# Feed-forward input projections: two 256-column matmuls on the same weights become one of 512 columns, and the halves are added outside TensorE

## The reference

```python
FFN_HIDDEN = 2816

def _swiglu(h, w_in, w_out):
    gate, up = jnp.split(h @ w_in, 2, axis=-1)
    return (jax.nn.silu(gate) * up) @ w_out

def _sublayer(x, fn, mod_j, g, b, weight):
    shift, scale, gate = mod_j[:, 0, None, :], mod_j[:, 1, None, :], mod_j[:, 2, None, :]
    y = fn(x * (1 + scale) + shift)
    return _layernorm(DEEPNORM_ALPHA * x + weight * gate * y, g, b)
```

## Time and profile before

| | |
|---|---|
| median of 3 runs | 3108.59 us (3104.44 to 3113.85) |
| the profiled execution | 3112.86 us |
| its span (first to last instruction) | 3111.0 us |
| TensorE busy | 2752.4 us, 88% of the span |
| VectorE busy | 1968.1 us, 63% |
| ScalarE busy | 1237.7 us, 40% |
| GpSimd busy | 1422.2 us, 46% |
| granted TensorE clock, mean | 0.913 of full speed |

### The profile page before, as it was taken

One profiled execution on the slowest core, in us unless ns is written; L12 is line 12 of the kernel. 1 busy time (PEld: TensorE's weight loads), 2 busy tenths in 40 slices (PEclk: granted clock), 3 DMA queues, 4 the chain that ended last, 5 costly groups with the idle time before them and its releaser, 6 DMA issues.

```text
span 3111.0 us, 49422 instructions
## 1 busy us (share of the span) xinstructions
PE 2752.4 (88%) x20583; PEld 2600.7 (84%) x20583; DVE 1968.1 (63%) x2280; ACT 1237.7 (40%) x1358; POOL 1422.2 (46%) x1126
## 2 busy tenths in 40 slices
PE   3998789999976999999789999999779979779797
PEld 3998679999965999998764999999669968468797
DVE  5657766676658666656766765766765454754553
ACT  2444444444444444434232444444444334334342
POOL 0890949579293692984730098494550000000000
PEclk7998989999987999999865999999889989789898
DMA  7765558667462675866620486675535535033452
GB/s 267 267 245 161 190 176 267 214 226 265 162 238 82 214 269 178 266 241 200 207 83 1 160 273 236 211 262 203 187 108 178 187 133 175 24 99 131 139 177 108
DMA packets 357173, 576.21 MB, mean 185 GB/s; under 512 B 22255, under 2 KB 297898, under 8 KB 356906
## 3 DMA queue, kind: packets, MB, share of 16 engines
q1 hardware_dynamic: 357034, 574.29, 54.2%
HBM read 573.20 MB, written 1.05 MB: 185 GB/s over the span
## 4 chain that ended last, share of the span: by engine, by line
PE 71%; DVE 13%; POOL 5%; ACT 4%; issue 4%; DMA 3%; SPq 1%; POOLq 0%; DVEq 0%; ACTq 0%
PE ps L1663 59%; PE ps L1716 3%; POOL mod_acc L647 3%; ACT whi L674 2%; PE ps L1722 1%; PE ps L2051 1%; POOL mod_w L642 1%; DVE wlo L1040 1%; DMA raw<-in_ffn_w_in_dram 1%; PE ps L2042 1%; DVE conv L1479 1%; PE ps L1773 1%; DVE z L1201 1%; DVE z L1179 1%; DMA raw<-in_ssm_w_in_dram 1%
## 5 line engine op out<-in xcount | busy, mean ns | idle before, releaser
L1040 DVE TENSOR_TENSOR wlo<-raw,whi 128x2048 fp32r<-128x2048 f32 x387 | 978.6, 2532 | 657.0 <-ACT whi L674 655.6
L1663 PE MATMUL ps<-H_hi,whi 128*128 128x256 f32 x3840 | 1099.4, 286 | 60.2 <-DVE conv L1479 21.8
L1663 PE MATMUL ps<-H_lo,whi 128*128 128x256 f32 x3840 | 1094.4, 285 | 0.0
L1663 PE MATMUL ps<-H_hi,wlo 128*128 128x256 f32 x3840 | 1094.0, 285 | 0.0
L674 ACT ACTIVATE whi<-raw 128x2048 fp32r<-128x2048 f32 (+1 forms) x402 | 759.9, 1892 | 645.6 <-DMA raw<-in_ffn_w_in_dram 259.7
L1663 PEld LDWEIGHTS ps<-H_hi,whi 128*128 128x128 f32 x3840 | 745.3, 194 | 68.6 <-issue 40.9
L647 POOL TENSOR_TENSOR mod_acc<-mod_acc,mod_w 128x512 f32<-128x512 f32 x450 | 793.0, 1788 | 0.0
L1663 PEld LDWEIGHTS ps<-H_lo,whi 128*128 128x128 f32 x3840 | 745.5, 194 | 0.2
L1663 PEld LDWEIGHTS ps<-H_hi,wlo 128*128 128x128 f32 x3840 | 745.1, 194 | 0.0
L1663 PE MATMUL ps<-A_hi,whi 128*128 (+1 forms) x1880 | 537.1, 286 | 21.0 <-DVE wlo L1040 21.0
L1663 PE MATMUL ps<-A_hi,wlo 128*128 (+1 forms) x1880 | 534.9, 285 | 0.0
(11 more groups left out here) (318 smaller groups left out, 2777.2 us busy)
## 6 DMA issues: line engine op xcount, KB each, us to landing
raw<-in_ffn_w_in_dram SPq DMA_DIRECT2D x176, 1024.0 KB, 5.3
mod_w<-in_w_mod_dram SPq DMA_DIRECT2D x180, 768.0 KB, 5.3
raw<-in_ffn_w_out_dram SPq DMA_DIRECT2D x88, 1024.0 KB, 4.8
raw<-in_w_gate_up_dram SPq DMA_DIRECT2D x22, 1024.0 KB, 5.1
raw<-in_ssm_w_in_dram SPq DMA_DIRECT2D x20, 1024.0 KB, 6.9
raw<-in_w_in_dram SPq DMA_DIRECT2D x14, 1024.0 KB, 5.1
raw<-in_diff_w_in_dram SPq DMA_DIRECT2D x12, 1024.0 KB, 7.7
raw<-in_w_down_dram SPq DMA_DIRECT2D x11, 1024.0 KB, 4.8
```

Of the source, the lines that this page charges most:

```text
L1040: tt(wlo[b % RAW][:, r], raw[b % RAW][:, r], whi[b % RAW][:, r].bitcast(F32), ALU.subtract).then_inc(w_lo, 1)
L1663: m = pe.matmul(out, l, r, start=first and i == 0, stop=last and i == 2, skip_group_check=rest)
```

## The change

In the input projection of all nine feed-forward parts, `columns` is replaced by `wide`. `H_hi` and `H_lo` become the two halves of one tile `H_two`. One matmul of 512 columns (a whole bank) multiplies `whi` by both: whi x H_hi goes to columns 0 to 255 of the bank and whi x H_lo to columns 256 to 511. The matmul wlo x H_hi stays one of 256 columns and adds to the first half. So 16 x 3 matmuls in a block become 16 x 2. Blocks 0 and 1, in `opening`, keep their three matmuls of 256 columns, the third now writing to the second half.

The two halves of a bank must then be added. ScalarE copies the second halves to SBUF (`low_part`, into `sg` or `am`), VectorE adds the first halves (`add_halves`), and only this addition frees the banks. Silu now runs on `sg` in SBUF, one turn later, and the product of gate and up has both inputs in SBUF. The output projection and all other stages are as before.

```diff
+        H_two = at("H_two", [P, 2, DC, S], o_hh, F32R)
+        H_hi, H_lo = H_two[:, 0], H_two[:, 1]
...
                 def gate(i, it=None):
 
                     p = g.p + i
+                    v = plan.free_val[p]
+                    act.wait_ge(banks_free[p % 2], v if it is None else 2 * it + v)
+                    nc.scalar.activation(sg[:, i // 2 % 2], sg[:, i // 2 % 2], ACT.Silu).then_inc(s["gated"], 1)
+
+                def low_part(i, it=None):
+                    j, p = i // 2, g.p + i
+                    reader, dst = (("multiplied", sg), ("a_lo", am))[i % 2]
+                    if j >= 2:
+                        v = n[reader] + j - 1
+                        act.wait_ge(s[reader], v if it is None else 2 * it + v)
                     u = g.l + 2 * (i + 1)
                     act.wait_ge(products, u if it is None else 8 * it + u)
-                    nc.scalar.activation(sg[:, i // 2 % 2], ps[:, bank(p):bank(p) + 2, 0:S], ACT.Silu)\
-                        .then_inc(banks_free[p % 2], 1)
+                    copy(dst[:, j % 2], ps[:, bank(p):bank(p) + 2, S:2 * S]).then_inc(s["low_out"], 1)
...
                 def turn(i, it=None):
                     convert(g.b + i + 2, it)
-                    if i % 2 == 0:
-                        gate(i, it)
+                    if i % 2 == 1:
+                        gate(i - 1, it)
+                    low_part(i, it)
                     if i % 2 == 0 and i >= 2:
                         product_hi(i // 2 - 1, it)
...
+                def add_halves(dst, i, it):
+
+                    p = g.p + i
+                    v = n["low_out"] + i + 1
+                    dve.wait_ge(s["low_out"], v if it is None else 4 * it + v)
+                    tt(dst, dst, ps[:, bank(p):bank(p) + 2, 0:S], ALU.add).then_inc(banks_free[p % 2], 1)
+
                 def product(j, it=None):
-
+                    add_halves(am[:, j % 2], 2 * j + 1, it)
                     p = g.p + 2 * j + 1
...
-                    tt(am[:, j % 2], sg[:, j % 2], ps[:, bank(p):bank(p) + 2, 0:S], ALU.mult).then_inc(banks_free[p % 2], 1)
+                    v = plan.free_val[p]
+                    dve.wait_ge(banks_free[p % 2], v if it is None else 2 * it + v)
+                    v = n["gated"] + j + 1
+                    dve.wait_ge(s["gated"], v if it is None else 2 * it + v)
+                    tt(am[:, j % 2], am[:, j % 2], sg[:, j % 2], ALU.mult).then_inc(s["multiplied"], 1)
...
                     if i % 2 == 1:
                         product(i // 2, it)
+                    if i % 2 == 0:
+                        add_halves(sg[:, i // 2 % 2], i, it)
...
+            def wide(g, i, it=None):
+
+                b, p = g.b + i, g.p + i
+                wait_banks(p, it)
+                wait_split(b, 0, it)
+                for h in range(2):
+                    for c in range(2):
+                        both = ps[:, bank(p) + c, :]
+                        for k in range(4 * h, 4 * h + 4):
+                            r = slice(k * 256 + c * P, k * 256 + c * P + P)
+                            if k == 0:
+                                pe.matmul(both, whi[b % RAW][:, r], H_two[:, :, k, :], start=True, stop=False)
+                            m = pe.matmul(both[:, 0:S], wlo[b % RAW][:, r], H_hi[:, k, :], start=False, stop=False, skip_group_check=True)
+                            if k:
+                                m = pe.matmul(both, whi[b % RAW][:, r], H_two[:, :, k, :], start=False, stop=k == DC - 1)
+                    m.then_inc(products, 1)
```

More of the change, by code:

```diff
@@ L167 @@
     "init": dict(c_turned=1, vec_turned=2, vec_ready=3, cond_ready=1, z_in=1, mod_sum=1, angle=1, rope_sin=2, lam_sum=1, lam_exp=1, picked=1, hf=4, h_hi=4, h_lo=4, ax_ready=1),
-    "ffn": dict(a_hi=FP, a_lo=FP),
+    "ffn": dict(low_out=2 * FP, gated=FP, multiplied=FP, a_hi=FP, a_lo=FP),
     "ln": dict(z_ready=8, zsum=6, squared=8, sqsum=6, ln_tok=1, ln_sum=1, ln_var=1, var=1, std=1, inv=1, rstd=1, centred=4, rstd_out=1, mod_hi=1, mod_lo=1, mod_row=1, mod_turn=1, mod_sum=1, hf=8, h_hi=8, h_lo=8, ax_ready=1),
@@ L373, in program @@
         A_hi, A_lo = at("A_hi", [P, FC, S], o_ah, F32R), at("A_lo", [P, FC, S], o_al, F32R)
-        H_hi, H_lo = at("H_hi", [P, DC, S], o_hh, F32R), at("H_lo", [P, DC, S], o_hl, F32R)
+        H_two = at("H_two", [P, 2, DC, S], o_hh, F32R)
+        H_hi, H_lo = H_two[:, 0], H_two[:, 1]
         ax = at("ax", [P, DC, S], room(4 * DC * S))
@@ L801, in turn @@
                     convert(g.b + i + 2, it)
-                    if i % 2 == 0:
-                        gate(i, it)
+                    if i % 2 == 1:
+                        gate(i - 1, it)
+                    low_part(i, it)
                     if i % 2 == 0 and i >= 2:
                         product_hi(i // 2 - 1, it)
-                walk(act, g, turn)
+                walk(act, g, turn, 4)
                 product_hi(FP - 1)
@@ L1268, in dve_ffn @@
                 g = st.lin["in"]
+                def add_halves(dst, i, it):
[3 more added lines that the diff above has]
+                    tt(dst, dst, ps[:, bank(p):bank(p) + 2, 0:S], ALU.add).then_inc(banks_free[p % 2], 1)
                 def product(j, it=None):
+                    add_halves(am[:, j % 2], 2 * j + 1, it)
                     p = g.p + 2 * j + 1
-                    v = plan.free_val[p - 1]
-                    dve.wait_ge(banks_free[(p - 1) % 2], v if it is None else 2 * it + v)
-                    u = g.l + 4 * (j + 1)
-                    dve.wait_ge(products, u if it is None else 8 * it + u)
-                    tt(am[:, j % 2], sg[:, j % 2], ps[:, bank(p):bank(p) + 2, 0:S], ALU.mult).then_inc(banks_free[p % 2], 1)
+                    v = plan.free_val[p]
[3 more added lines that the diff above has]
+                    tt(am[:, j % 2], am[:, j % 2], sg[:, j % 2], ALU.mult).then_inc(s["multiplied"], 1)
                 def product_lo(j, it=None):
@@ L1700, in whole, with opening @@
                 pe.wait_ge(s["h_lo"], st.n["h_lo"] - st.parts + k * st.parts // DC + 1)
-            def opening(st, g):
+            def opening(st, g, low=0):
                 for i in range(2):
@@ L1716, in opening @@
                                 pe.matmul(ps[:, bank(g.p + i) + c, 0:S], w[(g.b + i) % RAW][:, r], H_hi[:, k, :],
-                                          start=k == 0 and w is whi, stop=False)
+                                          start=k == 0 and w is whi, stop=low > 0 and k == DC - 1 and w is wlo)
                     whole(st, k)
@@ L1721, in opening @@
                             r = slice(k * 256 + c * P, k * 256 + c * P + P)
-                            m = pe.matmul(ps[:, bank(g.p + i) + c, 0:S], whi[(g.b + i) % RAW][:, r], H_lo[:, k, :], start=False, stop=k == DC - 1)
+                            m = pe.matmul(ps[:, bank(g.p + i) + c, low:low + S], whi[(g.b + i) % RAW][:, r], H_lo[:, k, :], start=False,
+                                          stop=k == DC - 1, skip_group_check=low > 0)
                             if k == DC - 1:
@@ L1841, in pe_ffn @@
                 g = st.lin["in"]
-                opening(st, g)
-                walk(pe, g, lambda i, it: None if it is None and i < 2 else columns(g, i, H_hi, H_lo, it))
+                opening(st, g, S)
+                walk(pe, g, lambda i, it: None if it is None and i < 2 else wide(g, i, it))
                 project(st, A_hi, A_lo, s["a_lo"], n["a_lo"], 2)
```

5 lines of the change are left out of this document (2 added, 3 removed).

## The result

The changed kernel takes 3120.03 us, the median of 20 runs (3112.57 to 3125.83), beside 3108.44 us of the kernel before (20 runs). The ratio is 1.0031, 95% interval 1.0021 to 1.0041. So it is slower by 0.3%. The medians lie 11.6 us apart (0.37%), where the forecast was +4.3 us.

What follows compares the result with a forecast made beforehand. TensorE was taken as the bound, its matmuls 0.1202 us apart with other work hidden. -29.9 + 22.3 + 1.6 + 11.9 - 1.6 = +4.3 us on the median 3108.6 gave 3112.9 us, range 3096 to 3134.

Steps and rivals of the forecast that it cites:

- merged pair, 180 blocks: Input projection, twenty blocks in nine parts: each block 0.166 us shorter with merged matmuls, 29.9 us saved.
- pause, seven parts with a carry: Block 2 starts late because VectorE's addition stands behind the carry: 2.64 to 3.80 us a part, 22.3 us together.
- pause, first and ninth part: No carry there, only the addition and a hop behind the copy: 0.8 us each, 1.6 us.
- clock after the pause: TensorE's clock falls behind the pause at block 2: 1.7 us in each of seven parts, 11.9 us.
- wait of the fourth part: TensorE's one wait on a late weight block goes, since it arrives 5 us later: 1.6 us back.
- late weight blocks: None in the sum; a rival had GpSimd hold back weights, block 28 late in six parts, 3124 us, chance 0.14.
- Who frees the banks: At block 2, VectorE's addition behind the carry frees the banks in place of ScalarE: 22.3 us plus 1.6 us.
- The clock: Pauses of 3.2 to 4.3 us before block 2 lower TensorE's clock, 11.9 us; rival that it holds, 3101, chance 0.12.
- The merged matmul: Input projection: a 512-column matmul takes 0.230 us, a merged pair saves 0.0104, 29.9 us; rival saving nothing, 3143, chance 0.08.
- The rest is hidden: Steady-state blocks: banks free 1.6 us after a block's end, needed at 5.6, or 2.9 entering the output projection; no cost.
- 6.5 us to spare: Second part's block 28: converted at 578.9, needed by TensorE at 585.4.
- 8.2 are to spare against 4.4: Block 28, with TensorE's delay counted: 8.2 us spare against GpSimd's 4.4 us lateness from ten products of 0.44 each.

Runs made afterwards that it cites:

- Experiment 3: Changed kernel with VectorE's addition of block 0 moved between z and ax of the carry; 3124.39 us, ratio 1.0031 to the kernel before.
- experiment 9: Changed kernel with high and low part of each depth piece side by side, so 512 moving columns are one stretch; 3122.35 us, ratio 1.0035 to before.
- experiment 4: Changed kernel with an odd block's product reading PSUM, the low part of up left out of the computation; 3115.45 us, ratio 1.0005 to before.
- Experiment 11: Experiment 6 with narrow matmuls directly behind each other and wide ones too, in place of alternating; 3084.99 us, ratio 0.9920 to the kernel before.
- experiment 2: Changed kernel with twelve 512-column matmuls into an unused bank, filling the pause in the seven parts with a carry; 3112.22 us, ratio 0.9995 to before.
- experiment 5: Changed kernel with the edits of experiments 3 and 4 together; 3096.74 us, ratio 0.9951 to the kernel before.
- Experiment 7: Changed kernel with only the fourteen w_mod requests of a feed-forward part spread over blocks 6 to 30; 3117.06 us, ratio 1.0023 to before.
- experiment 6: Experiment 3 with the fourteen w_mod requests in a feed-forward part at blocks 6 to 30 in place of 5 to 27; 3089.52 us, ratio 0.9933 to before.
- experiment 8: Kernel before the change with only the w_mod requests spread over blocks 6 to 30, as a control; 3108.72 us, ratio 0.9994.
- experiment 1: Changed kernel with only the merge undone, three matmuls of 256 columns for each product; 3136.49 us, ratio 1.0065 to the kernel before.

## Why the prediction was right, and where it was not

The forecast put the time at 0.14% over before, the measurement at 0.31%, just past the bound of 0.3% that it had set for "no change"; the interval holds both sides of that bound. The range held the time. Term by term, from the two traces:

| term | forecast | measured |
|---|---|---|
| merged pair, 180 blocks | -29.9 | -23.3 |
| pause, seven parts with a carry | +22.3 | +22.3 |
| pause, first and ninth part | +1.6 | +1.5 |
| clock after the pause | +11.9 | +10.8 |
| wait of the fourth part | -1.6 | -1.6 |
| late weight blocks | 0 | +5.4 |
| other stages | 0 | -4.5 |
| sum | +4.3 | +10.6 |

The spans differ by 10.7. The openings' own lengths, which the table leaves out, come to under 1 us. The last term is the variation from profile to profile and no effect of the change; by the medians the difference is 11.6. The two real misses, 6.6 us for the pair and 5.4 for late blocks, add up, and each is larger than the forecast of +4.3. That the result lies so near is partly luck.

**Who frees the banks** was right in mechanism and size. The row on which it rests, the end of the carry, decides. In all seven parts block 2 starts 17.5 us after `opening` does, whatever `opening` itself takes (12.9 to 14.1 us). So the pause differs from 3.4 to 4.6 us, and the carry is what sets it. Experiment 3 took it away, all but the 0.8 us for the addition and its hop, by moving one instruction. That both sums are 22.3 is luck: they move with the openings' lengths, and the pauses of the nine parts add up to 28.5 to 32.8 in the kernels that keep them, where this one has 31.1.

**The clock** was right in its mechanism, and its size was near. Five parts lost 1.6 us each. The eighth, with the longest pause (4.63 us), lost 2.8. That the sum came out near is luck, since it hangs on the lengths of seven pauses: by the same reading it is 3.2 us in experiment 9 and 13 in experiment 4. The sixth, with the shortest (3.38 us), lost nothing, as two windows of the changed kernel show, the pause and the 4 us behind it:

```profile
1785.20:1788.60 3.40, 0.31 (x3) 0.11 (x1) 3.40 (x11) 2.49 (x3) 0.59 (x2) 1.00 0.63 194
1788.60:1792.60 4.00, 3.99 (x23) 3.50 (x24) 3.97 (x3) 2.94 (x3) 4.00 (x4) 1.00 1.07 353
```

**The merged matmul** is the term that was mis-sized: "16 x (0.230 + 0.1202) = 5.60 us, 0.166 less" for a block. Measured is 112.70 / 20 = 5.635, 0.130 less. I had taken each width's pace from a stretch of its own kind. Alternating, a wide one takes 235.2 and a narrow one 117.0 ns, 2 ns more for a pair than expected. Experiment 11 shows that it is the alternation: sorted, the pair takes 350.3 to 350.7 by the length of an input stage, near the forecast's 350.2, and the stages, at 112.2, save 28 us. Experiment 9 excludes the address pattern. What in the alternation costs is open. The rule of the Trainium skill ("TensorE: Matmul & The Clock Gate", section "Back-to-back issue gap") that I weighed against the rows, with 216 and 109 ns for an isolated matmul, fits neither arrangement.

**The rest is hidden** holds the step that failed: "6.5 us to spare", and with TensorE's delay "8.2 are to spare against 4.4". The 4.4 is near: the last request comes 4.8 us later in parts 2 to 5, behind eleven products where the forecast counted ten (experiment 4). What is left of the spare is right there too: block 28's conversion took 2.3 to 2.8 us in the first five parts and ended 2.9 to 4.1 us before TensorE wanted it, where the forecast's numbers leave 3.8. The step that failed is "converted at 576.57 + 2.31", one part's row taken for all. In the sixth and seventh parts that conversion took 5.25 and 6.00 us, held up by GpSimd's three additions, and there block 28 was late by 2.4 and 1.3 us. The load had also landed later, in the sixth part because the request came 136.9 us after `ax`, in the seventh because it took 7.63 us in place of 6.2 to 6.6. But with a conversion of 2.3 neither would have been late. The other runs say the same: in experiments 2, 3, 5 and 9 block 28 was late once each, and each time its conversion took 5.87 to 5.98 us. The forecast saw the two engines exclude each other and counted it against GpSimd alone.

The other two waits, in the first and the sixth part, are of a second kind. TensorE goes on only 0.97 and 0.67 us after the matmul before, at the entry of the output projection, for an addition. VectorE's rows in the first part:

```profile
184.94 2.58 DVE L1050 TENSOR_TENSOR wlo<-raw,whi 128x2048 fp32r<-128x2048 f32 x1 [5.36 <-ACT whi L675]
...
189.81 3.38 DVE L1050 TENSOR_TENSOR wlo<-raw,whi 128x2048 fp32r<-128x2048 f32 x1
...
194.82 2.28 DVE L1050 TENSOR_TENSOR wlo<-raw,whi 128x2048 fp32r<-128x2048 f32 x1
197.03 0.68 DVE L1285 TENSOR_TENSOR am<-am,ps 128x512 f32<-128x512 f32 x1
```

VectorE had stood idle 5.36 us for a late block, and the conversions it then caught up on stood ahead of the addition. The forecast gave that addition 1.6 us against a cover of 2.9, and counted no conversion in it. Experiment 7 removes all four by the spreading alone, so all hang on the requests. Without the product from SBUF one wait is left in each of experiments 4 and 5, in other places, so the price for GpSimd decides most of them and not all.

**What would have changed the sign** wasn't in the forecast. It treated the pause as a cost and GpSimd's delay as a risk, side by side. Experiments 2, 3, 5 and 6 show that they hang together. The pause hid the delay: with it taken away alone, 26 us go and 28 us of waits come, nothing won (experiment 3). With pause, late requests and alternation all removed, the kernel is 0.8% faster than before (experiment 11), and experiment 8 shows that the spreading alone gives none of it.

## What to carry to other kernels

- Before an addition is given to another engine, look at what that engine is doing at the moment when the result is wanted. Here one VectorE instruction of 0.68 us, standing behind a carry, cost 22 us, and 11 more by the clock.
- When a wait is taken away and nothing is won, look for what it was hiding: follow the next wait of the bounding engine back to the queue, and see what the load stands behind. Here it was a request for other data that waits for a third engine; moving it by some blocks cost nothing and freed the gain.
- A spare that is read from one place holds for that place. Take the smallest over all parts and over all blocks behind the same kind of request, and take each instruction in it at its longest: here a conversion of 2.3 us had a case of 6.0 beside GpSimd.

## What the runs showed of the hardware

- Matmuls of two widths with changing weights cost more when they alternate than when they are sorted: 352.2 against 350.3 ns for one of 512 and one of 256 columns. A 256-column matmul steps by 120.2 ns in the kernel before, and by 117.0 (alternating) or 117.6 (sorted) where wide ones are near.
- A 512-column matmul whose moving columns lie in two stretches of 256 takes as long as one from a single stretch (235.2 ns both).
- Five kernels have the seven long pauses unfilled (the changed one and experiments 1, 4, 7 and 9). From one matmul's start to the next, 12 pauses of 3.4 to 3.6 us cost no clock, 18 of 3.7 to 4.5 us cost 1.4 to 1.6 us each, and 5 of 4.6 to 4.8 us 2.5 to 2.8. Filled with twelve matmuls whose result nobody reads, all seven kept the clock. In that kernel a shorter wait lowered it once: 2.58 us from one matmul's start to the next, for block 28 of the fifth part, with a granted clock of 0.60 in the 4 us from 1397. A wait of 2.51 us in the changed kernel's sixth part did not.
- A VectorE instruction of 512 elements with both inputs in SBUF took 1035 ns on average and eleven of them made GpSimd's last release in a part 4.8 us later, 0.44 each. One with an input in PSUM took 684 ns, and 22 of these in place of 11 (experiment 5) left it where it was before the change (129.7 to 130.5 us after `ax`, beside 129.6 to 130.0). The Trainium skill ("SBUF — State Buffer", section "SBUF: two separate sides") describes this as a lock; by that rule, the traces agree.
- It holds the other way too, and costs more there: a conversion of VectorE (128x2048, both inputs in SBUF) that stood beside three GpSimd additions in a row took 5.2 to 6.0 us in place of 2.3, and ended 2.15 us after the third of them at all six late blocks 28 of these kernels.
